# Sample attention of a hybrid decoder step: queries moved to partitions, four batches on column tiles of 32

## What is computed

```python
# stick-breaking, per batch b, head h, query q (8 of them), 264 keys s
z = q @ k.T * HEAD_DIM ** -0.5 + bias[h]
log_keep = where(mask, log_sigmoid(-z), 0)
log_remain = reverse cumulative sum of log_keep over later keys
a = where(mask, exp(log_sigmoid(z) + log_remain), 0);  o = a @ v
# dilated: three windows, merged by their denominators, which is one softmax over
s = q @ k.T * HEAD_DIM ** -0.5 - slope[h] * distance + log(number of windows that hold the key)
o = softmax(s) @ v
# both head groups, then
y = x + rmsnorm(concat(gate * headnorm(o)) @ w_out)
```

## Time and profile before

| what | value |
|---|---|
| median of 2 runs | 956.29 us (955.83 to 956.74) |
| the profiled execution | 955.46 us, span 953.7 us, mean granted TensorE clock 0.965 |
| busy over the span | PE 92%, DVE 61%, ACT 49%, POOL 34% |
| second stage | from 738.93 us to the end, 214.8 us |

### The profile page before, as it was taken

How to read it: one execution, slowest core, us unless ns; L and a number is a source line. 1 busy time by engine, 2 the same in 40 slices (tenths; PEclk the granted TensorE clock), 3 DMA queues, 4 the chain that set the end, 5 groups by cost and what they waited for, 6 DMA issues and landing times. The chain is left out here.

```text
span 953.7 us, 16337 instructions
## 1 busy us (share of the span) xinstructions
PE 876.2 (92%) x5526; PEld 779.6 (82%) x5526; DVE 577.1 (61%) x1171; ACT 463.6 (49%) x901; POOL 328.6 (34%) x279
## 2 busy tenths in 40 slices
PE   4999899999898999979899998999876999999995
PEld 3888899899788989968799997888765788888874
DVE  4657876667686776667767757787686222222222
ACT  6426565444756544565645447565476122222221
POOL 3326542232554222263542215563045122222211
PEclk9999999999999999989999999999897699999998
DMA  8131202133112212211221321121273435555301
GB/s 264 45 99 53 75 23 69 32 91 102 36 56 62 74 32 82 84 53 32 82 78 37 90 76 60 32 82 46 79 272 115 136 110 162 175 165 176 95 23 45
DMA packets 112327, 83.44 MB, mean 87 GB/s; under 512 B 7858, under 2 KB 106418, under 8 KB 111986
## 3 DMA queue, kind: packets, MB, share of 16 engines
q1 hardware_dynamic: 110578, 69.78, 24.4%
q10 hardware_dynamic: 1664, 12.58, 4.0%
HBM read 65.30 MB, written 25.43 MB: 95 GB/s over the span
## 5 line engine op out<-in xcount | busy, mean ns | idle before, releaser
L692 PE MATMUL proj_bank<-h_hi,w_hi 128*128 128x384 f32 (+1 forms) x768 | 278.3, 362 | 0.0
L694 PE MATMUL proj_bank<-h_hi,w_lo 128*128 128x384 f32 (+1 forms) x768 | 254.2, 331 | 0.0
L693 PE MATMUL proj_bank<-h_lo,w_hi 128*128 128x384 f32 (+1 forms) x768 | 253.7, 330 | 0.0
L1393 DVE TENSOR_TENSOR split<-sc_bank,split 128x512 fp32r<-128x512 f32 (+1 forms) x160 | 101.5, 634 | 113.3 <-ACT split L1077 112.5
L692 PEld LDWEIGHTS proj_bank<-h_hi,w_hi 128*128 128x128 f32 x768 | 147.2, 192 | 19.1 <-issue 15.9
L693 PEld LDWEIGHTS proj_bank<-h_lo,w_hi 128*128 128x128 f32 x768 | 147.5, 192 | 1.9 <-issue 1.9
L1657 POOL TENSOR_TENSOR work<-work 128x896 f32<-128x896 f32 (+7 forms) x64 | 92.5, 1448 | 161.7 <-DVE work L1439 161.7
L1077 ACT ACTIVATE split<-sc_bank 128x512 fp32r<-128x512 f32 (+1 forms) x160 | 87.8, 549 | 123.8 <-PE sc_bank L795 121.1
L694 PEld LDWEIGHTS proj_bank<-h_hi,w_lo 128*128 128x128 f32 x768 | 146.4, 191 | 0.0
L795 PE MATMUL sc_bank<-consts,work 128*128 128x128 f32 x576 | 93.1, 281 | 20.7 <-ACT work L1098 13.5
L815 PE MATMUL o_bank<-split,v_st 128*128 128x256 f32 x320 | 88.0, 296 | 18.3 <-DVE split L1393 18.1
(11 more groups left out here) (153 smaller groups left out, 1481.7 us busy)
## 6 DMA issues: line engine op xcount, KB each, us to landing
w_raw<-in_w_in_dram SPq DMA_DIRECT2D x64, 256.0 KB, 2.9
out_dram<-stage SPq DMA_DIRECT2D x32, 192.0 KB
work<-in_x_prompt_dram SPq DMA_DIRECT2D x8, 512.0 KB, 8.2
tables<-in_c_prompt_table_dram ACTq DMA_DIRECT2D x8, 512.0 KB, 4.0
out_dram<-in_cache_k_dil_dram ACTq DMA_DIRECT2D x8, 512.0 KB, 4.3
out_dram<-in_cache_v_dil_dram ACTq DMA_DIRECT2D x8, 512.0 KB, 4.0
kc<-in_cache_k_sb_dram SPq DMA_DIRECT2D x64, 64.0 KB, 1.9
vc<-in_cache_v_sb_dram SPq DMA_DIRECT2D x64, 64.0 KB, 1.9
```

Of the source, the lines that this page charges most:

```text
L692: mm(o, w_hi[s][:, k, :], h_hi[:, k, c0:c0 + n_all], start=(k == 0), stop=False)
L693: mm(o, w_hi[s][:, k, :], h_lo[:, k, c0:c0 + n_all], start=False, stop=False)
L694: last = mm(o, w_lo[s][:, k, :], h_hi[:, k, c0:c0 + n_all], start=False, stop=(k == NK - 1))
L1393: ve.tensor_tensor(a_lo[:, k % 2, 0:n], turn_bank(name, ("T", k))[:, 0:n], a_hi[:, k % 2, 0:n].bitcast(F32), ALU.subtract).then_inc(low_se ...
```

## The change

The chain has queries on the partitions instead: head h, query q of batch b stand in row 32 x + 8 h + q, with b = 4 r + x, for r = 0, 1 and x = 0 to 3; 16 of each 32 rows are in use. The scores of a batch are one fp32 matmul with the 32 query columns as weights and 256 key columns moving, whose result goes to the partitions 32 x to 32 x + 31, and one with the 8 new keys. The sums over later keys are two scans of DVE along the row. The weights (of the attention) are transposed by TensorE for both kinds of heads, copied to `ut` (by ACT) and `un` (by DVE), and are the stationary side: 24 fp32 matmuls with 128 value columns moving, again in groups of four with results on 32 partitions each; 8 of these have 8 rows. The result `ot` is transposed back (`sample_back`). The output matmuls stand between these groups in blocks. SP issues the transfer of the first new values later, and the values of chain n+2 now wait for `sample_back`. In the last phase of the first stage DVE computes a bias by row (`s_bias`) and clears `q_bd`; a fill with ones and a copy `k_s` go.

```diff
-                sp.dma_start(v_new[:, br, :], rows_s[br][1][:, :, i * P:i * P + P]).then_inc(v_in[br], 16)
+                src = rows_s[br][1][:, :, i * P:i * P + P].rearrange("b t c -> t b c")
+                sp.dma_start(v_new[:, br], src).then_inc(v_in[br], 16)
             def load_terms(i):
-                sp.dma_start(s_table[:], c_sample_table[i:i + 1].rearrange("a p x n -> (a p) x n")).then_inc(s_table_in, 16)
+                sp.dma_start(s_table[:], c_sample_table[i]).then_inc(s_table_in, 16)
...
-            load_new(0, 0)
...
+            load_new(0, 0)
...
-            def sample_scores(j, between):
+            def sample_scores(j):
+                i, br = j // 2, j % 2
                 pe.wait_ge(kct_set, 4 * j + 4)
                 pe.wait_ge(qbd_set, j + 1)
-                past = proj_bank[:, 0, 0:256].rearrange("p (g h b q) -> p g h b q", g=2, h=2, b=DB)
...
-            def sample_sums(j):
...
-            def sample_turn(j, back):
...
+                for r in range(2):
+                    for x in range(4):
+                        b, rows = 4 * r + x, slice(32 * x, 32 * x + 32)
+                        mm(proj_bank[rows, r, 0:256], q_bd[:, b, :], kct[:, 2 * b:2 * b + 2, :], start=True, stop=True)
+                    for x in range(4):
+                        b, rows = 4 * r + x, slice(32 * x, 32 * x + 32)
+                        last = mm(proj_bank[rows, r, 256:264], q_bd[:, b, :], samp[:, i + 4 * br, 1, b * DS:b * DS + DS],
+                                  start=True, stop=True, skip_group_check=True)
                 last.then_inc(s_pe, 1)
-            def sample_values(j, bank, between):
+            def sample_turn(j):
+                if j % 2 == 0:
+                    pe.wait_ge(s_act, 4 * j + 3)
+                else:
+                    pe.wait_ge(s_dve, 6 * j + 3)
+                for r in range(2):
+                    for g in range(2):
+                        mm(proj_bank[:, 0, (2 * r + g) * P:(2 * r + g) * P + P], zs[:, r, g * P:g * P + P], ident,
+                           start=True, stop=True, is_transpose=True)
+                for r in range(2):
+                    last = mm(proj_bank[0:DS, 1, r * P:r * P + P], zs[:, r, 256:264], ident, start=True, stop=True, is_transpose=True)
+                last.then_inc(s_pe, 1)
+            def sample_values(j):
                 br = j % 2
-                pe.wait_ge(s_act, 3 * j + 3)
+                pe.wait_ge(s_act, 4 * j + 4)
+                pe.wait_ge(s_dve, 6 * j + 4)
                 pe.wait_ge(v_in[br], V_LOADS[br] * 16 * (j // 2 + 1))
-                o = bank.rearrange("p (h n) -> p h n", h=2)
...
+                for r in range(2):
+                    for g in range(3):
+                        for x in range(4):
+                            b, rows = 4 * r + x, slice(32 * x, 32 * x + 32)
+                            w, v = (ut[:, 2 * r + g, rows], vcs[br][:, 2 * b + g, :]) if g < 2 else (un[:, r, rows], v_new[:, br, b, :])
+                            last = mm(o_bank[rows, 0, r * P:r * P + P], w, v, start=(g == 0), stop=(g == 2), skip_group_check=True)
+                last.then_inc(s_pe, 1)
+            def sample_back(j):
+                pe.wait_ge(s_dve, 6 * j + 5)
+                for r in range(2):
+                    last = mm(o_bank[:, 0, 256 + r * P:256 + r * P + P], ot[:, r, :], ident, start=True, stop=True, is_transpose=True)
+                last.then_inc(s_pe, 1)
...
-                sample_scores(j, lambda x: output(b, x // 2, (x + 1) // 2))
+                sample_scores(j)
+                output(b, 0, 8)
                 if n == 0:
                     small_group(2 * NPAIR + 1, "M", 1, None, None)
-                if j % 2 == 0:
...
+                output(b, 8, 24)
+                sample_turn(j)
+                output(b, 24, 32)
+                sample_values(j)
+                if j < 7:
+                    turn_keys(j + 1, (0, 1))
+                output(b, 32, 38)
+                sample_back(j)
                 if n == 0:
                     pe.wait_ge(rooted, 4 * 8 + 3)
-                if j == 7:
+                if j < 7:
+                    turn_keys(j + 1, (2, 3))
+                    output(b, 38, 48)
+                else:
+                    output(b, 38, 44)
                     pe.wait_ge(s_root, 1)
                     mm(o_bank[:, 1, :], head_mean, t_all[:].rearrange("p e n -> p (e n)"), start=True, stop=True).then_inc(s_root, 1)
-                    output(b, 38, 43)
...
+                    output(b, 44, 48)
...
-                act.wait_ge(s_dve, 5 * j + 1)
-                av(es[:], es[:], ACT.Exp).then_inc(s_act, 1)
-                act.wait_ge(s_act, 3 * j + 1)
-                av(es[:], es[:], ACT.Ln, bias=one_c[:, 0:1]).then_inc(s_act, 1)
+                act.wait_ge(s_dve, 6 * j + 1)
+                if j % 2 == 0:
+                    av(es[:], zs[:], ACT.Exp).then_inc(s_act, 1)
+                    act.wait_ge(s_act, 4 * j + 1)
+                    av(es[:], es[:], ACT.Ln, bias=one_c[:, 0:1]).then_inc(s_act, 1)
+                    return
+                for r in range(2):
+                    av(es[:, r], zs[:, r], ACT.Exp, scale=-1.0, bias=small[:, r:r + 1],
+                       accum_out=small[:, 2 + r:3 + r]).then_inc(s_act, 1)
             def sample_weights(j):
-                act.wait_ge(s_dve, 5 * j + 4)
...
-            def sample_exp(j):
...
-            def sample_copy(j):
...
+                if j % 2 == 0:
+                    act.wait_ge(s_dve, 6 * j + 3)
+                    av(zs[:], zs[:], ACT.Exp).then_inc(s_act, 1)
+                act.wait_ge(s_pe, 4 * j + 2)
+                av(ut[:].rearrange("p x n -> p (x n)"), proj_bank[:, 0, :], ACT.Copy).then_inc(s_act, 1 if j % 2 == 0 else 2)
...
-                if j % 2 == 0:
...
+                sample_soften(j)
                 if n >= 1:
                     output_norm(n - 1)
+                sample_weights(j)
                 if j == 7:
...
+                q = samp[:, j // 2 + 4 * (j % 2), 0, :].rearrange("p (b n) -> p b n", b=DB)
+                ve.tensor_copy(q_bd[0:HD, :, 0:DS], q[0:HD])
+                ve.tensor_copy(q_bd[HD:P, :, DS:2 * DS], q[HD:P]).then_inc(qbd_set, 1)
+            def sample_terms(j):
                 i, br = j // 2, j % 2
-                q = samp[:, i + 4 * br, 0, :]
...
-            def sample_terms(j):
...
                 if br == 0:
-                    ve.memset(zs[HD:P, 2, :], -FAR)
                     dve.wait_ge(s_pe, 4 * j + 1)
-                    for h in range(2):
...
-            def sample_linear(j):
...
-            def sample_subtract(j):
+                    b = s_bias[:, 1, i:i + 1]
+                    new = s_mask[:, 0:DS].rearrange("p (a n) -> p a n", a=1).to_broadcast((P, 2, DS))
+                    ve.tensor_scalar(zs[:, :, 0:256], proj_bank[:, :, 0:256], b, LINEAR, ALU.add, ALU.min)
+                    ve.scalar_tensor_tensor(zs[:, :, 256:264], proj_bank[:, :, 256:264], b, new, ALU.add, ALU.min).then_inc(s_dve, 1)
+                    return
+                dve.wait_ge(s_table_in, 16 * (i + 1))
+                dve.wait_ge(s_pe, 4 * j + 1)
+                for r in range(2):
+                    ins = ve.tensor_tensor_reduce(out=zs[:, r], in0=proj_bank[:, r, 0:264], in1=s_table[:], scale=1.0,
+                                                  scalar=3.0 * FAR, op0=ALU.add, op1=ALU.min, accum_out=small[:, r:r + 1])
+                ins.then_inc(s_dve, 1)
+            def sample_shares(j):
+                dve.wait_ge(s_act, 4 * j + 2)
+                if j % 2 == 0:
+                    for r in range(2):
+                        back = es[:, r][:, ::-1]
+                        ins = ve.tensor_tensor_scan(back, back, back, 0.0, ALU.add, ALU.max)
+                    ins.then_inc(s_dve, 1)
+                    dve.wait_ge(s_dve, 6 * j + 2)
+                    ve.tensor_tensor(zs[:], zs[:], es[:], ALU.subtract).then_inc(s_dve, 1)
+                    return
+                ve.reciprocal(small[:, 2:4], small[:, 2:4]).then_inc(s_dve, 1)
+                dve.wait_ge(s_dve, 6 * j + 2)
+                for r in range(2):
+                    ins = ve.tensor_scalar(zs[:, r], es[:, r], small[:, 2 + r:3 + r], None, ALU.mult)
+                ins.then_inc(s_dve, 1)
+            def sample_result(j):
+                dve.wait_ge(s_pe, 4 * j + 2)
+                ve.tensor_copy(un[:].rearrange("p r n -> p (r n)"), proj_bank[0:DS, 1, 0:2 * P]).then_inc(s_dve, 1)
                 dve.wait_ge(s_pe, 4 * j + 3)
-                ve.tensor_tensor(us[:].rearrange("p x n -> p (x n)"), zs[:].rearrange("p x n -> p (x n)"),
...
-            def sample_min(j):
...
-            def sample_normal(j):
...
-            def sample_result(j, bank):
+                ve.tensor_copy(ot[:].rearrange("p r n -> p (r n)"), o_bank[:, 0, 0:2 * P]).then_inc(s_dve, 1)
                 dve.wait_ge(s_pe, 4 * j + 4)
-                out = o_all[:, j // 2 + 4 * (j % 2), :]
```

(41 more changed lines are left out.)

131 lines of the change are left out of this document (23 added, 108 removed).

## The result

| what | before | after |
|---|---|---|
| median | 956.29 us | 916.39 us (915.73 to 917.05, 2 runs) |
| ratio to before, 95% interval | | 0.9571 (0.9556 to 0.9587) |
| the profiled execution | 955.46 us, span 953.7 | 917.05 us, span 915.2 |
| from the first score matmul to the end | 214.8 us | 173.9 us |

The kernel is 4.3% faster. 926 us was forecast; the measured time is 9.6 us under that and inside the range.

The account below looks back on a forecast made before the run. TensorE's own work was taken to bound the kernel. The terms summed as 955.46 - 25.4 - 6.2 + 1.0 + 1.0 = 925.9, so 926 us was predicted, range 911 to 950.

Parts of the forecast that it names:

- tiles 1 to 6: Second stage, its middle tiles: 18.5 us each against 22.73, together -25.4 us.
- tile 0: Second stage, first tile: 14.5 us kept at 1.2 GHz, 25.5 us against 31.74, so -6.2 us.
- tile 7, its clock, the last stage: Second stage's end: tile 19.0 against 19.91 us with 4.1 idle, 1.5 for clock, 0.4 for last stage: +1.0 us.
- end of the first stage: DVE's work there: a fill and a copy go, two small operations come; +1.0 us (0 to 2.6).
- The quarter: Scores and values: four matmuls on four groups of output columns run together, 2.7 us a tile instead of 10.7.
- no overlap: Rival: the four matmuls of a group run in turn, 8.0 us more per tile, 993 or 982 us; chance 0.09.
- two at once: Rival: only two matmuls of a group run together, 2.7 us more in each tile, 948 us; chance 0.12.
- The wait for `un`: TensorE ahead of the values: waits 0.8 us for DVE's copy, slightly less in dilated tiles; bounds 0 and 1.5.
- The 8-column matmuls: Scores with the new keys: 8 small matmuls at 0.23 each, 1.8 us unoverlapped, or 0.05 each in the lower case.
- The changes of form: TensorE, scores, transposes and values: nine changes between forms of the array per tile at 0.17 each, 1.5 us.
- my own sign: TensorE's waits: about 0.8 us for `un` per tile, 4 in tile 7; a wait before the transposes refutes the chain's order.
- SP's queue: SP's transfers: unchanged work, near 14 us per tile of 18.5; cost nothing while tiles stay over 15 us.

Follow-up runs that it names:

- e_one_tile: Changed kernel, but the four matmuls of each group (scores and values) write to the same 32 output columns, partitions 0 to 31: 969.17 us.
- e_two_tiles: Changed kernel, but the four matmuls of each group write to two column tiles only, partitions 0 to 31 and 32 to 63: 936.56 us.
- e_un_last: Changed kernel, but in the values the two groups with 8 rows of weights stand behind the four groups with 128 rows: 915.43 us.
- e_prepare_late: Changed kernel, but DVE prepares the next chain's queries behind the copy `un` instead of ahead of it: 913.95 us.
- e_best: Changed kernel with early gates, tile 7 outputs moved back, `prepare` behind `un`, `s_bias` ahead of tile 0, 8-row groups adjacent, ACT's tile 0 order swapped: 898.56 us.
- e_before_dense: Kernel before, but tile 0's first 8 output matmuls stand ahead of the 16 score matmuls instead of between them: 956.33 us.
- e_gates_early: Changed kernel, but the gates are computed in tiles 1, 3 and 5 behind the chain's result, instead of tile 7 ahead of `un`: 911.61 us.
- e_tail: Changed kernel with gates in tiles 1, 3 and 5, and in tile 7 21 instead of 4 outputs behind the product with `head_mean`: 905.93 us.

## Why the prediction was right, and where it was off

| term | forecast | measured | why |
|---|---|---|---|
| tiles 1 to 6 | -25.4 | -32.3 | 17.35 us a tile for 18.5 |
| tile 0 | -6.2 | -10.2 | the clock came back after 3 us, not 14; a wait of 1.84 takes part of it back |
| tile 7, its clock, the last stage | +1.0 | +1.7 | tile 7 -0.6, last stage +2.3 |
| end of the first stage | +1.0 | +2.3 | 1.3 by the wait for DVE, 1.6 from before it, -0.5 behind it |
| sum, from 953.7 | -29.6 | -38.5 | 915.2 |

The sum of the prediction gives 925.9 for the profiled execution; the 0.8 by which the median lies above it was named and not added, so 926 should have been 926.7. The 1.6 us at the end of the first stage, there already one wait earlier (719.25 for 717.63), are within what runs with the same first stage differ by.

**The quarter** was the step on which all hung, and `e_one_tile` and `e_two_tiles` show it. The earlier trace rows were the right row to lean on. The rivals are out: no overlap was measured at 969 us (I had 982 to 993: the 8-column ones cost 0.06 each, as the lower end had it, and a tile took 24.0 us where that end made 25.1), two at once at 937 (I had 948, by 2.7 us a tile where it was 2.15). The Trainium skill's page TensorE: Matmul & The Clock Gate has 2.38 times for three column tiles (Part 3, measured speedup); here four gave 3.9 on 256 columns. Its rule in the same part is that a weight load overlaps running matmuls only if the row groups differ. By it the rival without overlap would hold, as the prediction says. The runs disagree: four column tiles of the same rows cost what one costs.

**Tiles 1 to 6** were 1.15 us better each. The wait for `un` was 0.36 in the mean for 0.8: it is 0.71 in stick-breaking tiles, near the forecast, but none in dilated tiles. There POOL's residual ends 8.77 us behind the start of the tile (tile 1: 769.14 + 2.39 - 762.76), in stick-breaking ones 9.45 (tile 2: 786.87 + 2.40 - 779.82), and `un` is ready in time. I had written "slightly less" without working the dilated chain out. The 8-column matmuls were about 0.12 for the 0.45 in my quarter. The changes of form cost 0.13 each where `e_un_last` measured them and 0.10 around the scores, for my 0.17. The mechanism, `prepare` held by POOL's residual, was as forecast (`e_prepare_late`).

**Tile 0** is the term that was wrong in its reason. I kept 14.5 us at 1.2 GHz because before had them, as if the slow stretch were given. The stretch was 3.1 us (741.26 to 744.4), and 11.4 us less at half clock are 5.7 us. Of these 1.84 went to the wait ahead of the transposes, which by my own sign refutes my order of the chain. It does so in tile 0 alone: there ACT does the prompt's last norm ahead of the chain's exp and ln, which I had not counted, and in `e_best`, where they change places, the wait is gone. 25.5 - 5.7 + 1.8 = 21.6; measured 21.5. Before, the clock stood at 0.50 from 738.93 to 753 us. Windows of the changed kernel, the clock in the last column but two:

```profile
741.26:744.00 2.74, 2.74 (x34) 1.83 (x35) 0.57 (x1) 0.42 (x2) 2.69 (x2) 0.50 0.80 251
745.00:752.00 7.00, 5.60 (x23) 3.93 (x21) 2.29 (x5) 2.85 (x5) 0.00 (x0) 1.00 0.64 180
```

TensorE was busy through the slow stretch in both. What differs is what it does: before, two 16-column matmuls to one output; after, wide matmuls. `e_before_dense` makes this likely but not settled: it moves the clock up and down in one tile, but in no run was the number of columns varied alone.

**Tile 7** waited 3.41 us for 4.1, for the reason given (`e_gates_early`). The clock, which I had put at 1.5 (0 to 5), cost 1.6 in the outputs of tile 7 (`e_gates_early`) and more in the last stage. That had 4 outputs behind `head_mean` where before had 10, and so waited 4.31 for 1.68. The wait itself cost nothing, since `y_lo` came 6.36 us behind `head_mean`, before 6.72. What it cost is the clock behind it: from 892.48 to 898.20 outputs step 0.43, twelve of them, 12 x 0.20 = 2.4 us; in `e_tail`, where the wait is 0.45, there are none. I had read only tile 7 of the order, not what stands behind `head_mean`.

**SP's queue** cost nothing, as forecast, even at 16.8 us a tile (`e_best`).

## What to carry to other kernels

Before adding up small matmuls, look at what their results occupy: here four with 32 columns of weights, each to its own 32 partitions, cost what one costs, and another order within a group of eight changed 0.02 us. Once TensorE's work shrinks, list for each new wait what stands ahead of the releasing instruction on its engine: here a copy, four gate steps and two tiny bias operations, none of them needed by the instruction that stood behind them, cost 11 us. And don't carry a slow-clock stretch over from the kernel before: when the instructions in it change, work it out anew, and read the stretches that were not touched, too, since the clock can fall there.
